# Gated block of a state-space mixer: half of the first block as float32 products, placed into the recurrence

## The reference, cut to what matters

```python
u = h @ in_w
bu = jnp.einsum('gnp,blgp->lbgn', b_bar, ug)          # 128 groups x 64 states
_, states = lax.associative_scan(combine, (a_seq, bu), axis=0)
y = jnp.real(jnp.einsum('gpn,lbgn->blgp', cmat, states)).reshape(Bsz, L, D)
y = y + d_skip * u
g = jax.nn.gelu(y).astype(h.dtype)
z = g @ glu_w + glu_b                                   # glu_w: 2048 x 4096
val, gate = jnp.split(z, 2, axis=-1)
return val * jax.nn.sigmoid(gate)
```

## Time and profile before

| | us |
|---|---|
| three runs, median | 2499.35 |
| lowest, highest | 2496.43, 2507.01 |
| profiled execution, its own time | 2497.91 |
| span of that execution | 2496.2 |
| PE busy | 2395.9 |
| VectorE busy | 1864.2 |

### The profile page before, as it was taken

One profiled execution on the slowest core, in us unless ns is written; L12 is line 12 of the kernel. 1 busy time (PEld: TensorE's weight loads), 2 busy tenths in 40 slices (PEclk: granted clock), 3 DMA queues, 4 the chain that ended last, 5 costly groups with the idle time before them and its releaser, 6 DMA issues.

```text
span 2496.2 us, 33093 instructions
## 1 busy us (share of the span) xinstructions
PE 2395.9 (96%) x12489; PEld 1928.5 (77%) x12489; DVE 1864.2 (75%) x2972; ACT 1053.9 (42%) x1250; POOL 35.4 (1%) x67
## 2 busy tenths in 40 slices
PE   5797799999999999999999999999999999999998
PEld 3475378878888888888878888778888888888886
DVE  6377988978778887889878987887787755455457
ACT  4254034464443444344464444464644444444442
POOL 0000000000000000000000000000000000000000
PEclk9898799999999999999999999999999999999999
DMA  8995948858888998899758877736698766656674
GB/s 305 359 338 181 368 141 288 296 186 289 299 284 292 339 323 275 281 322 328 254 166 282 280 268 226 223 105 200 221 302 293 229 194 191 188 186 197 191 221 142
DMA packets 314686, 627.36 MB, mean 251 GB/s; under 512 B 30656, under 2 KB 31072, under 8 KB 314272
## 3 DMA queue, kind: packets, MB, share of 16 engines
q1 hardware_dynamic: 310240, 611.35, 73.0%
q0 software_dynamic: 4288, 13.90, 2.0%
HBM read 623.05 MB, written 2.10 MB: 250 GB/s over the span
## 4 chain that ended last, share of the span: by engine, by line
PE 84%; DVE 9%; DMA 3%; ACT 2%; issue 1%; SPq 1%; DVEq 0%; ACTq 0%
PE psA L2055 40%; PE psB L2055 39%; DVE prod L1398 2%; DMA col_raw<-in_ada_w 1%; DVE tmp L1403 1%; DVE st L1409 1%; PE psT L1687 1%; DMA w_raw<-in_ffn_w_in 1%; PE psM L1719 1%; DVE w_lo L1077 0%; DMA Cnat_im<-in_s_c_im 0%; DMA w_raw<-in_s_glu_w 0%; ACT w_hi L757 0%; DVE w_lo_more L1077 0%; ACT stgA L854 0%
## 5 line engine op out<-in xcount | busy, mean ns | idle before, releaser
L1077 DVE TENSOR_TENSOR w_lo<-w_raw,w_hi 128x1024 fp32r<-128x1024 f32 x740 | 902.8, 1223 | 497.7 <-ACT w_hi L757 493.3
L757 ACT ACTIVATE w_hi<-w_raw 128x1024 fp32r<-128x1024 f32 x740 | 783.1, 1060 | 1119.4 <-PE psB L2055 492.0
L2055 PE MATMUL psB<-w_hi,hT_hi 128*128 128x512 f32 x1040 | 406.8, 391 | 0.0
L2055 PE MATMUL psB<-w_hi,hT_lo 128*128 128x512 f32 x1040 | 404.9, 389 | 0.0
L2055 PE MATMUL psB<-w_lo,hT_hi 128*128 128x512 f32 x1040 | 404.6, 389 | 0.0
L2055 PE MATMUL psA<-w_hi,hT_hi 128*128 128x512 f32 x1008 | 398.0, 395 | 5.3 <-DVE w_lo L1077 2.0
L2055 PE MATMUL psA<-w_hi,hT_lo 128*128 128x512 f32 x1008 | 393.3, 390 | 0.0
L2055 PE MATMUL psA<-w_lo,hT_hi 128*128 128x512 f32 x1008 | 393.0, 390 | 0.0
L1094 DVE SCALAR_TENSOR_TENSOR ada_acc<-ada_raw,csil,ada_acc 128x512 f32<-128x512 f32 x450 | 336.2, 747 | 12.8 <-DVE ada_acc L1094 0.5
L2055 PEld LDWEIGHTS psB<-w_hi,hT_hi 128*128 128x128 f32 x1040 | 195.2, 188 | 43.5 <-issue 2.8
L2055 PEld LDWEIGHTS psA<-w_hi,hT_hi 128*128 128x128 f32 x1008 | 189.7, 188 | 50.3 <-issue 8.1
(11 more groups left out here) (370 smaller groups left out, 2303.1 us busy)
## 6 DMA issues: line engine op xcount, KB each, us to landing
w_raw<-in_ffn_w_in SPq DMA_DIRECT2D x352, 512.0 KB, 4.6
ada_raw<-in_ada_w SPq DMA_DIRECT2D x480, 256.0 KB, 5.3
w_raw<-in_ffn_w_out SPq DMA_DIRECT2D x176, 512.0 KB, 4.7
col_raw<-in_ada_w SPq DMA_DIRECT2D x128, 512.0 KB, 6.5
w_raw<-in_dsa_in_w SPq DMA_DIRECT2D x112, 512.0 KB, 4.6
w_raw<-in_s_glu_w SPq DMA_DIRECT2D x64, 512.0 KB, 5.1
w_raw<-in_s_in_w SPq DMA_DIRECT2D x32, 512.0 KB, 6.8
w_raw<-in_dsa_out_w SPq DMA_DIRECT2D x32, 512.0 KB, 5.3
```

The lines of the kernel that those rows point to most:

```text
L757: nc.scalar.activation(high(u), w_raw[:, u % RING], ACT.Copy).then_inc(w_hi_ready, 1)
L1077: V.tensor_tensor(low(u), w_raw[:, u % RING], high(u).bitcast(F32), ALU.subtract).then_inc(w_lo_ready, 1)
L2055: ins = MM(PS[s][:, t, 0:r.width], a_[:, kt, tok], b_[:, kk, 0:r.width], start=kt == 0 and m == 0, stop=k == r.units - 1 and kk == UK - 1 ...
```

## The change

The `s = 0` half of the first gated block (`whole(r, i, s)`) is no longer formed of rounded parts. Its eight units land as they are in `glu_raw` (over `aT_hi` and `aT_lo`, which are free then), each with a semaphore of its own, and PE multiplies `uT` with them as float32: `whole_products(k, t)` for unit `k` and token tile `t`. Token tile 0 needs only pieces 0 and 1 and stands before the outputs of piece 2; token tile 1 stands behind them: units 0 and 1 between the outputs of pieces 2 and 3, units 2 to 7 after these. The rounding and splitting of these eight units is gone; `rounded(u)` makes the counters skip them.

The pieces' outputs now all go to `PS[1]` (first channel half) and `T` (second), so that `PS[0]` is free: for token tile 0 in its first bank, and for two of the four gate products and then token tile 1 in its second. GELU is applied piece by piece, four times 128 x 1024.

On PE, 22 column units come first, then the inside terms of pieces 0 and 1 with two column units behind every second row tile, then 14 column units, the outputs of piece 0 with eight units between, the last four; then the outputs of piece 1 in a row, gate products and inside terms of pieces 2 and 3. On SP the eight raw units follow the column units. The first column units are issued a little sooner. `g_high(k)` waits until the raw unit that lies where it writes has been used. The ada units of the run start at place 9 instead of 5.

```diff
-        glu = Run("glu", 4, s5_glu_w[0], (D, 0), dense=(EARLY, 3, 13, 5), before="s5")
+        glu = Run("glu", 4, s5_glu_w[0], (D, 0), dense=(EARLY, 3, 13, 9), before="s5")
...
+            def raw_unit(k):
+                row, col = k * UK * P, glu.col[0]
+                sp.dma_start(glu_raw[k][:], glu.w[row:row + UK * P, col:col + NB].rearrange("(k p) n -> p k n", p=P)
+                             ).then_inc(raw_landed[k], 16)
...
-                    sp.wait_ge(w_lo_ready, glu.unit)
-                    sp.wait_ge(ada_used, EARLY * AU)
                     for a in range(FRONT, COLS):
+                        m = a - FRONT
+                        if m < RING:
+                            sp.wait_ge(w_lo_ready, glu.unit - RING + m + 1)
+                        elif m == RING:
+                            sp.wait_ge(ada_used, EARLY * AU - ARING // 2)
                         col_unit(a)
+                    sp.wait_ge(bu_full, 8)
...
+                        if whole(r, i, n // r.units):
+                            raw_unit(n)
+                        elif r is glu and i == 0 and n < r.units + RING:
+                            sp.wait_ge(col_used, glu_after(n - r.units))
...
             def g_high(k):

-                act.wait_ge(gelu_done, 2 + k // 4)
+                act.wait_ge(gelu_done, 3 + k // 4)
+                act.wait_ge(w_used, glu.unit + 4 + k // 4 * 4)
...
                 gelu(0)
+                gelu(1)
                 act.wait_ge(col_used, COLS)
...
                 for n in range(RING):
-                    hi_unit(glu.unit + n)
-                gelu(1)
-                for k in range(4):
-                    g_high(k)
+                    hi_unit(glu.unit + glu.units + n)
                 gelu(2)
-                for k in range(4, 8):
+                gelu(3)
+                for k in range(8):
                     g_high(k)
...
                 vec.wait_ge(y_full, 2)
-                lo_unit(glu.unit)
-                lo_unit(glu.unit + 1)
-                g_low(0)
-                g_low(1)
-                lo_unit(glu.unit + 2)
-                g_low(2)
-                g_low(3)
-                lo_unit(glu.unit + 3)
-                for k in range(4, 8):
+                for n in range(RING):
+                    lo_unit(glu.unit + glu.units + n)
+                for k in range(8):
                     g_low(k)
...
+            def whole_products(k, t):
+
+                tok = slice(t * P, (t + 1) * P)
+                pe.wait_ge(gelu_done, 1 + 2 * t + k // 4)
+                pe.wait_ge(raw_landed[k], 16)
+                for kk in range(UK):
+                    kt = k * UK + kk
+                    ins = MM(PS[0][:, t], uT[:, kt, tok], glu_raw[k][:, kk], start=kt == 0, stop=kt == KT - 1)
+                return ins
...
-                col_units(FRONT, FRONT + 46)
+                units(22)
                 pe.wait_ge(bu_read_act, 24)
                 pe.wait_ge(diag_ready, 1)
-                outputs_inside(0)
-                outputs(0, FRONT + 46, 4)
-                col_units(FRONT + 54, FRONT + 56)
-                outputs_inside(1)
-                outputs(1, FRONT + 56, 4)
-                outputs_inside(2)
+                for f in range(KT):
+                    outputs_inside(f // 8, f)
+                    if f % 2:
+                        units(2)
+                units(14)
+                pe.wait_ge(rec, rec_after(0, HALF - 1))
+                for f in range(8):
+                    outputs(0, f)
+                    if f % 2:
+                        units(2)
+                units(FRONT + 64 - at_[0])
+                pe.wait_ge(rec, rec_after(1, HALF - 1))
+                for f in range(8, KT):
+                    outputs(1, f)
+                pe.wait_ge(gate_ready, 1)
+                gate(0)
+                gate(1)
                 pe.wait_ge(gelu_done, 1)
...
+                for f in range(8):
+                    outputs_inside(2, f)
+                gate(2)
+                gate(3)
+                pe.wait_ge(gelu_done, 2)
+                for f in range(8, KT):
+                    outputs_inside(3, f)
+                for k in range(glu.units):
+                    whole_products(k, 0)
+                pe.wait_ge(rec, rec_after(0, CHUNKS - 1))
+                for f in range(8):
+                    outputs(2, f)
                 pe.wait_ge(gate_done, 4)
-                outputs_inside(3)
-                outputs(2, 0, 0)
-                outputs(3, 0, 0)
+                for k in range(2):
+                    whole_products(k, 1).then_inc(w_used, 1)
+                pe.wait_ge(rec, rec_after(1, CHUNKS - 1))
+                for f in range(8, KT):
+                    outputs(3, f)
+                for k in range(2, glu.units):
+                    if k == 4:
+                        turn_row(2, M[:, 1], late_row)
+                    whole_products(k, 1).then_inc(w_used, 1)
```

More of the change, by code:

```diff
@@ L1907, in outputs @@
[L1907 to L1922 removed]
+                at0 = (f % 4 * 2 + d) * HALF
```

116 lines of the change are left out of this document (54 added, 62 removed).

## The result

The kernel after takes 2513.51 us (median of six executions, 2501.76 to 2518.68) against 2499.36 beside it: a ratio of 1.0043, 95% interval [1.0022, 1.0064]. It is slower, by 11 us by the ratio and 14 by the medians, and outside my range.

A forecast was written before the change was run, and what follows sets the result against it. TensorE, busy 96% of the span, bounds the kernel. A 4.4 us wait goes, 1.2 comes, 10 us hide under DMA, 6.7 are added, 7.3 move behind the stream: -0.5 us, median 2498.8 us, range 2490 to 2507.

The forecast's parts named there:

- What bounds the kernel: Whole span: TensorE is busy for 96% of it, so the end moves only where PE waits or its work shrinks.
- yardstick: Start of the gated block's first `s=1` product, 378.86 before, forecast 378.4; its shift goes to the end one to one.
- The products: First gated block's `s=0` half: 32 float32 products at 0.89 us, 28.5 us, replace 21.8 us; 6.7 us more PE work.
- the sum: PE's work added up through the state-space stretch: yardstick at 378.4 against 378.86, a move of -0.5 us.
- Rival 3: Whole products run at the 1.2 GHz level, 1.78 us each: +28 us for all; chance 0.04.
- The stream: Column units stay DMA-bound at 2.65 us a pair, hiding the inside terms; last pair starts at 310.8, ends at 311.7.
- The sum behind it: PE after the column units, from 311.7: gapless work except a 1.2 us GELU wait, reaching the yardstick at 378.4.
- Rival 2: Column stretch stays at 1.2 GHz, 4.4 us a pair, landed units giving back about 6: +7.5 us; chance 0.08.
- Rival 1: Last outputs: the recurrence still ends last, yardstick 367.7, -11.2 us; chance 0.16 in part, 0.05 in full.
- Rival 4: Gated block: VectorE is too late with more ada per place and later splits, +1 to +4 us; chance 0.10.

The follow-up runs named there:

- a1_again: The kernel after, unchanged, measured a second time: 2516.11 us, ratio 1.0068.
- c1: Kernel after plus nine unread products, piece 1 outputs and piece 2 inside terms in the column stream, whole products before the last inside terms: 2487.64 us, ratio 0.9951.
- c2: Kernel after plus 15 unread products, with the raw units held back until the outputs of piece 1 are done: 2498.36 us, ratio 0.9990.
- d1: c1 without any of its unread products: 2500.14 us, ratio 0.9984.
- b1: Kernel before with only the new placing of column units, inside terms and outputs; first block stays three float32r products: 2504.97 us, ratio 1.0021.
- d4: c1 unchanged, measured again: 2489.03 us, ratio 0.9962.
- a2: Kernel after plus 15 unread float32 products, one behind each pair of column units outside the inside terms: 2502.11 us, ratio 1.0014.
- d2: Kernel before plus one unread 512-column float32 product behind each of column-unit pairs 4 to 23: 2500.75 us, ratio 1.0001.
- c3: Kernel after plus unread products only behind column-unit pairs 4 to 11, ahead of the inside terms: 2499.59 us, ratio 1.0001.

## Why the prediction was wrong, step by step

**What bounds the kernel: right.** Large shifts of the yardstick went to the end nearly one to one: 15.6 us of yardstick and 14.9 of span between the profiles of a1_again and of the kernel after, 10.9 and 11.3 between before and c1. Over all profiles the span less the yardstick lies between 2115.8 and 2120.1 us, so shifts of a few us can't be followed to the end.

**The products: a little too dear.** From 337.68 to 351.56 are 13.88 us for 32 instructions, 0.434 us from start to start, where I had 0.446. Token tile 0 took 13.9 us, not 14.3. All 32 products and the four transposes took 27.9 us (13.88, 3.61 from 360.08 and 10.44 from 370.94), against 22.4 before: 5.5 us more, where the sum had 6.7. That PE's busy time rose by 6.8 us is luck, since it also counts column units at either level; a1, with the same instructions, has 2417.3 us. Rival 3 did not happen: no whole product ran low.

**The stream, in the short execution: right.** Pairs every 2.56 us in the mixture, last unit at 312.73 against 310.8. Of the 1.9 us, 1.4 are there before the first column unit (230.89 against 229.46), in code that the change doesn't touch.

**The sum behind it: small misses.** From 313.58 to 351.56 PE took 38.0 us, the sum 36.0 (311.7 to 347.7). A wait of 1.70 us on "issue" was not in it, nor that the gate products behind it ran low (1.87 us for two instructions, 1.12 in c2). I had looked for what the raw units' transfers wait for, and not for what waits for them. From there to the yardstick PE took 29.8 us, the sum 30.7. So 1.9 + 2.0 - 0.9 = 3.0 us make 381.38 of 378.4. The wait of 1.2 us before token tile 1 was met (1.20), though the profile names "issue" and not ScalarE for it; there was none on `st`, as forecast.

**Rival 2: this is the step that failed.** It had the right mechanism, and was given a chance of 0.08. The argument against it was "with the terms between them PE has no idle time at that level, and the trace shows the clock come back under steady work". Its first half is true in a1 (PE busy for 14.00 of 14 us), and the clock did not come back. Its second half rested on the earlier trace rows, 349.2 to 354, and these are state outputs. I carried what one kind of work did over to another. In d1 the state outputs bring it back here as well, within about 3 us (291.55 to 294), while the inside terms ahead of them had not in 35. A row of the kernel before could have warned me: there the terms at 288 ran fast behind a pair that was fast already, so that they said nothing of whether terms can raise the clock.

The Trainium skill, TensorE: Matmul & The Clock Gate, section "HAM oscillation — how this bites in real kernels", puts a low clock down to work in pieces with waits between. That is like the column units up to 252 (0.50 and 0.64, 8 of 12 us busy), though most of their waits (0.5 to 1.8 us) are shorter than the 3 to 5 us of the page's kernel. As I read it, the mixture, which has no waits, would run at full clock, and I leaned on that. a1, b1 and d1 show it at 0.50 for 28 us and more without a wait; the measurement decides.

**Its price was mis-sized too:** +7.5 us, against 15.6 of yardstick. 4.4 us a pair was near (4.62). The "units already landed give back about 6" was not. Eight times 2.06 us is 16.5, and this is the whole way from 2.2 us ahead at the eleventh pair to 14.3 us behind at the nineteenth. From there to the last pair the long execution took 36.0 us and the short one 35.6, so nothing came back; the stream is only 14.6 us later, and not 16.5, because it had been ahead. The bytes agree. In the three windows from 252 to 311, the long execution moved 299, 225 and 352 GB/s where the short one moved 406, 387 and 381: 28 x 107 + 14 x 162 + 17 x 29 = 5.8 MB less, which at 400 GB/s is 14.4 us. SyncE issues a unit only when PE has used the tenant of its place, so while PE lags the DMA engines, which bound the stream, are idle in part (share 0.67 and 0.68 in a1's windows from 266 on, where the short one has 1.03 and 1.00); the stock of landed units gave nothing back here. At 291.38 PE took three pairs at once and then waited 1.28, 2.53 and 3.01 us for the next.

**Rival 1** did not come about in the kernel after, and for the reason given: PE came to the last outputs at 363.69, 13.2 us behind the end of the recurrence (350.50 in this trace), where the sum had 10.7. c1 gave it its order, and the number I had worked out for it, 367.7, was met at 367.97. That it agrees this closely is partly luck: PE started the last outputs 1.2 us later than the 349.1 of that sum, and took 17.7 us from there where the sum had 18.6.

**Rival 4: not seen.** From the yardstick to the end of the span the short execution took 2118.7 us, the kernel before 2117.3, and two executions of one kernel, c1 and d4, 2116.9 and 2120.1: such differences are scatter.

**What stays open:** what in the inside terms keeps the clock down. State outputs have 64 columns as well and raise it. No run tells whether it is the width of the weights (128 against 32) or something else. Nor is it known why the level at 252 differs from one execution to the next of the kernel after: of ten, two were short. The traces show one part of it. Among column units with waits the level goes up and down: in a1 the pair at 249.30 was at full clock (1.06 us) and the one at 254.42 was not (1.94), in the kernel before, of the pairs from 234 to 287, only those at 249.55, 263.29, 273.49 and 287.00 were. The mixture meets whichever of the two is there when it starts, and holds it.

## What to carry to other kernels

Where TensorE waits for DMA and then goes over to short products, look at the clock at that edge, and don't count on steady work to raise it: price the stretch at both levels, and where the low one would make PE the bound, put a long product between the transfers while PE is idle anyway. When a stream is DMA-bound, count the bytes that are not moved; here they were lost to the end, whatever had landed. And work moved under a transfer pays only if what is then left behind it is shorter: the change left outputs and terms behind the stream that c1 put inside, and that was worth 14 us between the medians of a2 and c1.

## What the runs showed of the hardware

- The mixture of 64-column float32 products and column units is stable at either level: 2.56 us a round at 2.4 GHz (the short execution), 4.62 us at 1.2 GHz for 35 us without a gap on PE (a1).
- One unread 512-column product behind each DMA wait, about 0.9 us of PE in a gap of 1.5 us (2.56 less 1.06), holds the clock at 1.00 in a stretch that stands at 0.50 to 0.66 without it (240 to 288; a2 against a1, d2 against the kernel before). At the start of the stretch it can still be low for a few us: the window from 240 to 252 has 0.86 to 0.92 in c1, c2, c3 and d4.
- State outputs cost the same at either level: 64 of them take 1.80 us from start to start at 0.50 (d1, 291.55 to 293.35) and 1.77 at 1.00 (the kernel before, 293.50 to 295.27), where a pair of column units is recorded with 1.94 us against 1.06.
- With the DMA queues full (share 1.05), PE stood still twice, for 1.58 and 1.40 us, with no releaser; with them nearly empty (0.02) not at all (a2, c2).
